# One head stage of a hybrid mLSTM and attention layer: values evicted by ScalarE, mLSTM steps one point sooner, low weight parts by VectorE at fixed places

## The chip, the cores and the metric

The kernel runs on one core of one Trainium2 chip. The metric is device time in microseconds, as the median of several runs. TensorE multiplies (PE in the profile, with PEld for the loading of its stationary operand), VectorE is DVE, ScalarE is ACT, GpSimd is POOL, and SyncE (SP) issues most of the DMAs.

## The reference

One decoder layer on 1024 tokens of width 1024 in float32. What the change touches is the middle of it, one mLSTM head and one attention head of each of three groups at a time:

```
proj = h @ w_in[l]
xc = silu(causal_depthwise_conv(xa, w_conv[l], b_conv[l]))
q_m, k_m = xc_h @ w_q_mlstm[l], xc_h @ w_k_mlstm[l] * DH ** -0.5
h_m = sigmoid(oa) * mlstm_chunkwise(q_m, k_m, v_m, ia + b_igate, fa + b_fgate)
h_m = rms_norm(h_m, g_mlstm_head[l]) + skip_mlstm[l] * xc
y_m = (h_m * silu(za)) @ w_out_mlstm[l]
...
outs, lses = dilated_window_attention(qh, kh, vh, window, dilation)   # three groups
o_a = sum(softmax(lses) * outs)
y_a = (o_a * silu(zb)) @ w_out_attn[l]
```

There are 4 mLSTM heads of width 256, and 3 attention groups of 4 heads of width 128 (windows 128, 512, 2048; dilations 1, 4, 16).

## The kernel before

Each engine runs its own hand-written program, in order, and semaphores tie them together. The program has stages: setup, blocks (projections as sums of block products), `mix` (the four heads), and merge (output projections and the final norm). The change is in `mix` alone.

**Float32 in three passes.** Every weight chunk of 128x1024 is split into a high part (ACT copies it to a rounded type, `whi`) and a low part (`wraw - whi` into `wlo`, by POOL at L1239). A product is three matmuls: high by high, high by low, low by high (L590 to L592). The semaphore `w_high` counts the high parts, `w_split` the low parts. SP loads chunk q into `wraw[q % 2]` once the low part of chunk q-2 is done (`load`, L1142 to L1145). PE starts with a chunk once its low part is done.

**A head** has eight chunks, p = 0 to 7. p = 0, 1, 3, 4 are the token projections n = 0 to 3 (v and the output gate, 48 matmuls each, in `project_tokens`); p = 2 is the fold chunk (`fw`, the products of the q and k weights); p = 5, 6, 7 are n = 4, 5, 6 (ZA twice and ZB, 48 matmuls each, in `project`). So n = 2 needs the low part of p = 3. Call T the time at which PE begins n = 0 of a head.

**Points.** The 144 matmuls of n = 4, 5, 6 are cut into 24 parts of six, and behind each part (`point` u = 0 to 23) PE does a step of mLSTM and a step of attention. `SCORES`, `ATTEND`, `NORM` and `TURN` say at which u they begin. An mLSTM chunk takes two steps: `state_update` and `scores_and_keys` at the even one, `numerator` at the odd one. An attention group takes six steps x = 0 to 5: `turn_values` at x = 0, scores at x = 0 to 3, transposed probabilities (`p_turned`) at x = 1 to 4, products with the values at x = 2 to 5. ACT and DVE have a `mixing(u)` of their own. On DVE it does `head_out` (odd mLSTM step) or `state` and `weigh` (even step), then attention: the masks of the scores (L1739) and the copy of the transposed probabilities into `pT` (L1748, L1751). Behind u = 20 come `head_norm`, and behind the turned output `head_scaled`, `silu_za`, and then the next head's `conv(0)`.

**Around a head's start** DVE does: conv(0); the sigmoid gate of the previous head's z (`silu_zb`); `weigh_groups`, which waits once for ACT's exp; conv_gate(0); conv(1); conv_gate(1); the low parts of xc; the scaling and joining of the previous head's three attention outputs; `fold_low`; `intra_args`.

Of the kernel before, what the change touches and what calls it, by code (L numbers as in the profile page):

```python
# [9 lines left out]
P = 128  # L10
# [240 lines left out]
def buffers(sb, ctx, table):  # L251
# [28 lines left out]
    ("hin", [P, DH + 1], F32), ("hnb", [P, DH + 1], F32), ("small", [P, 4], F32), ("vr", [P, 6, NCH], F32), ("nm", [P, 2, 2], F32),  # L280
# [788 lines left out]
def mix(nc, a, sem, ps, T):  # L1069
# [52 lines left out]
    SCORES, ATTEND, NORM, TURN = 4, 3, 20, 23  # L1122
# [110 lines left out]
    def gpsimd(pool):  # L1233
        for q in range(HEAD0, MERGE0 + 2 * PLAIN):
            p = (q - HEAD0) % CHUNKS
            at = q % 2 if q >= MERGE0 else ring_slot((q - HEAD0) // CHUNKS, p - (p > FOLD))
            hi, to = (fw[:, 0, :], fw[:, 1, :]) if p == FOLD and q < MERGE0 else (whi[:, at, :], wlo[:, at, :])
            pool.wait_ge(w_high, q - 2)
            nc.gpsimd.tensor_tensor(to, wraw[:, q % 2, :], hi.bitcast(F32), ALU.subtract).then_inc(w_split, 1)  # L1239
# [5 lines left out]
    def tensor(pe):  # L1245
        t_ = nc.tensor
        for i in range(0, HEADS):
# [103 lines left out]
            def turn_output():  # L1351
                for j in range(4):
                    pe.wait_ge(normed, 2 * i + 2 + j // 2)
                    if j == 3:
                        pe.wait_ge(out_used, i * 4 + 5)
                    for c in range(4):
                        mm = t_.transpose((M0, M1, M2, M0)[j][:, c * P:(c + 1) * P],
                                          og[:, 4 * (j // 2) + c, (j % 2) * P:(j % 2 + 1) * P], ident[:])
                    mm.then_inc(out_turned, 1)
# [72 lines left out]
    def scalar(act):  # L1432
# [4 lines left out]
        for i in range(0, HEADS):  # L1437
# [78 lines left out]
            def intra_weights():  # L1516

                act.wait_ge(e_arg, i + 1)
                for c in range(NCH):
                    ins = A(ew[:, c, :], ew[:, c, :], ACT.Exp, bias=hc[:, i, 0, c:c + 1])  # L1520
                ins.then_inc(e_exp, 1)
# [21 lines left out]
            def root_table():  # L1543
                act.wait_ge(normed, 2 * i + 1)
                A(vr[:, 2, 0:1], one[:], ACT.Abs_reciprocal_sqrt).then_inc(root_done, 1)

            def attend(g, x):
                if x >= 2:
# [12 lines left out]
            def mixing(u):  # L1561
                m, at = mlstm_step(u), attend_step(u)
                if u == NORM - 1:
                    root_table()
                if m is not None and m % 2:
                    inter((m - 1) // 2)
                if at:
                    attend(*at)
                if m is not None and m % 2:
                    square((m - 1) // 2)  # L1570
# [17 lines left out]
            next_high(5)  # L1588
            fold_high()
            for j in range(4):  # L1590
                keep_tokens(0, j)
            for n in range(ZA, MAIN):
                for h in range(2):
                    for part in range(PARTS_OF):
# [4 lines left out]
                        if (n, h, part) == (ZA, 0, 1):  # L1599
                            for j in range(4):  # L1600
                                head_keep(j)
# [6 lines left out]
                        if u == NORM + 1:  # L1608
                            z_sigmoid(ZA)
                            z_sigmoid(ZA + 1)  # L1610
# [4 lines left out]
    def vector(dve):  # L1615
# [10 lines left out]
        for i in range(0, HEADS):  # L1626
            hp = hpa[:, i]

            def conv(q):
                dve.wait_ge(xa_in, 16 * i + 16)  # L1630
                if q:
                    dve.wait_ge(xc_done, i * 2 + 1)
                x = xa[:, q, :]
# [26 lines left out]
            def weigh(c):  # L1660
                dve.wait_ge(sk_out, i * 8 + c + 1)
                if c == 0:
                    dve.wait_ge(e_exp, i + 1)
# [29 lines left out]
            def head_norm():  # L1693
# [9 lines left out]
                for h in range(2):  # L1703
                    cs = slice(4 * h, 4 * h + 4)
                    v.tensor_tensor(og[:, cs], og[:, cs], vr[:, 5, cs].unsqueeze(2).broadcast_to([P, 4, DH]), ALU.mult).then_inc(normed, 1)  # L1705
                for q in range(2):
                    step(v.tensor_scalar(xc[:, q, :], xc[:, q, :], hp[:, q, 5:6], None, ALU.mult))

            def head_scaled():
                for j in range(4):  # L1710
# [3 lines left out]
                    v.scalar_tensor_tensor(part_, (M0, M1, M2, M0)[j], hp[:, q, 6:7], part_, ALU.mult, ALU.add).then_inc(out_used, 1)  # L1714

            def silu_za(q):
                dve.wait_ge(z_sig, i * 3 + q + 1)
                z = (cv, sg)[q]
                step(v.tensor_tensor(z[:], z[:], tn[1 - q], ALU.mult))
                if q == 0:  # L1720
                    dve.wait_ge(out_used, i * 4 + 8)
                v.tensor_tensor(xc[:, q, :], xc[:, q, :], z[:], ALU.mult).then_inc(um_done, 1)
# [5 lines left out]
            def attend(g, x):  # L1728
                if x == 0:
                    for j in range(2):  # L1730
                        dve.wait_ge(v_turned, i * 6 + 2 * g + j + 1)
                        v.tensor_copy(vt[:, 4 * j:4 * j + 4, :], (A1, A2)[j].rearrange("p (c e) -> p c e", c=4)).then_inc(v_kept, 1)  # L1732
# [62 lines left out]
            def mixing(u):  # L1795
                m, at = mlstm_step(u), attend_step(u)
                if m is not None and m % 2:
# [17 lines left out]
            conv_gate(0)  # L1815
            conv(1)
            conv_gate(1)
# [4 lines left out]
            if i:  # L1822
                scale_two(i - 1)
                join_two(i - 1)
                join_third(i - 1)
# [6 lines left out]
            silu_za(0)  # L1832
            silu_za(1)
# [532 lines left out]
```

## Time and profile before

| | |
|---|---|
| Time, median of 3 runs | 1391.75 us (1391.37 to 1392.53) |
| Profiled execution: time | 1391.71 us |
| Profiled execution: span | 1389.7 us |
| PE busy | 1354.6 us, 97% |
| DVE busy | 863.7 us, 62% |
| ACT busy | 561.1 us, 40% |
| POOL busy | 448.3 us, 32% |
| The head stage | about 575 to 1119 us |

The span is what the profiler saw of the core's work, and the time of that execution is 2.0 us more. The granted PE clock is full (2.4 GHz) in all 40 slices of the page, and the mean over the span is 0.999. A matmul's end is modelled, so durations of neighbours overlap: a 128x512 matmul is listed at 0.39 us, and the next starts 0.23 us after it. Where an interval is wanted, the starts are to be read.

### The profile page before, as it was taken

The page shows a single profiled execution, that of the slowest core. Times are in us where ns is not written, and L with a number is a line of the kernel's source. Part 1 is how long each engine was busy: PE and PEld are TensorE (multiplying, and loading weights), DVE is VectorE, ACT ScalarE, POOL GpSimd, SP SyncE. Part 2 cuts the span into 40 slices and gives each one's busy share as a digit, 9 for nine tenths or more (in the row PEclk, how much of TensorE's full clock was granted, in tenths as well). Part 3 has the DMA queues.
Part 4 walks back from the last instruction along what each step waited for, and adds up shares of the span by engine and source line. Part 5 has one row for each costly group of instructions (what it writes and reads, how often), then busy time and mean ns, then how long its engine had stood idle before and what let it go on. Part 6 is the DMA issues. An engine that isn't in the chain of part 4 may idle for free.

```text
span 1389.7 us, 17404 instructions
## 1 busy us (share of the span) xinstructions
PE 1354.6 (97%) x6477; PEld 1132.2 (81%) x6477; DVE 863.7 (62%) x1474; ACT 561.1 (40%) x980; POOL 448.3 (32%) x288
## 2 busy tenths in 40 slices
PE   8999999999999999999999999999999899999998
PEld 6888888888888888888877887888788787888886
DVE  7888765664734554345677567665866566433586
ACT  7664343344444444234343434444444335111122
POOL 0196555454544555420022002200220021222551
PEclk9999999999999999999999999999999999999999
DMA  8512322332324433462218311730272056354543
GB/s 333 190 62 101 129 108 105 122 121 94 118 101 142 152 137 139 168 177 59 52 47 232 89 30 48 242 92 16 76 213 61 17 204 236 107 179 154 178 137 106
DMA packets 64334, 176.31 MB, mean 127 GB/s; under 512 B 21906, under 2 KB 22034, under 8 KB 62199
## 3 DMA queue, kind: packets, MB, share of 16 engines
q1 hardware_dynamic: 59962, 162.44, 35.2%
q10 hardware_dynamic: 3168, 8.70, 1.9%
q0 software_dynamic: 1120, 4.06, 1.0%
q8 instruction: 52, 0.85, 0.3%
q14 instruction: 32, 0.25, 0.1%
HBM read 130.39 MB, written 44.79 MB: 126 GB/s over the span
## 4 chain that ended last, share of the span: by engine, by line
PE 83%; DVE 8%; ACT 4%; DMA 4%; issue 1%; SPq 0%; POOL 0%; ACTq 0%; DVEq 0%
PE banks L590 24%; PE banks L592 24%; PE banks L591 24%; DMA wraw<-in_w_all 3%; PE banks L1391 2%; PE banks L1381 1%; PE banks L1341 1%; PE banks L1347 1%; PE banks L1400 1%; PE banks L582 1%; PE banks L554 1%; ACT whi L1465 1%; PE banks L1339 1%; DVE vt L1732 1%; DVE og L1705 1%
## 5 line engine op out<-in xcount | busy, mean ns | idle before, releaser
L590 PE MATMUL banks<-h_hi,whi 128*128 128x512 f32 x584 | 234.9, 402 | 0.0
L1239 POOL TENSOR_TENSOR wlo<-wraw,whi 128x1024 fp32r<-128x1024 f32 x32 | 78.1, 2442 | 485.4 <-ACT whi L1465 458.3
L592 PE MATMUL banks<-h_hi,wlo 128*128 128x512 f32 x584 | 228.1, 391 | 0.0
L591 PE MATMUL banks<-h_lo,whi 128*128 128x512 f32 x584 | 227.6, 390 | 0.0
L714 POOL TENSOR_TENSOR wlo<-w_sum,whi 128x512 fp32r<-128x512 f32 x104 | 154.4, 1487 | 127.1 <-ACT whi L839 127.1
L590 PE MATMUL banks<-t_hi,whi 128*128 128x512 f32 x416 | 161.8, 389 | 0.0
L591 PE MATMUL banks<-t_lo,whi 128*128 128x512 f32 x416 | 161.8, 389 | 0.0
L592 PE MATMUL banks<-t_hi,wlo 128*128 128x512 f32 x416 | 161.8, 389 | 0.0
L985 DVE TENSOR_TENSOR c_sum<-c_sum,banks 128x512 f32<-128x512 f32 x182 | 124.8, 686 | 42.5 <-PE banks L592 29.7
L592 PEld LDWEIGHTS banks<-h_hi,wlo 128*128 128x128 f32 x584 | 109.6, 188 | 23.5
L839 ACT ACTIVATE whi<-w_sum 128x512 fp32r<-128x512 f32 x104 | 65.4, 630 | 153.9 <-PE banks L592 93.1
L591 PEld LDWEIGHTS banks<-h_lo,whi 128*128 128x128 f32 x584 | 109.9, 188 | 20.5
L590 PEld LDWEIGHTS banks<-h_hi,whi 128*128 128x128 f32 x584 | 109.8, 188 | 20.4
L590 PE MATMUL banks<-whi,h_hi 128*128 128x512 f32 x256 | 99.9, 390 | 0.0
L592 PE MATMUL banks<-whi,h_lo 128*128 128x512 f32 x256 | 99.7, 389 | 0.0
L591 PE MATMUL banks<-wlo,h_hi 128*128 128x512 f32 x256 | 99.6, 389 | 0.0
L592 PEld LDWEIGHTS banks<-t_hi,wlo 128*128 128x128 f32 x416 | 78.1, 188 | 16.2
L590 PEld LDWEIGHTS banks<-t_hi,whi 128*128 128x128 f32 x416 | 78.1, 188 | 16.2
L591 PEld LDWEIGHTS banks<-t_lo,whi 128*128 128x128 f32 x416 | 78.1, 188 | 16.1
L861 ACT ACTIVATE fin<-c_sum 128x1024 f32<-128x1024 f32 x52 | 75.5, 1501 | 2.6 <-DMA chunk_decay_rows<-wlast 2.6
L714 POOL TENSOR_TENSOR wlo<-wraw,whi 128x512 fp32r<-128x512 f32 x39 | 58.2, 1500 | 44.7 <-ACT whi L839 44.7
L714 POOL TENSOR_TENSOR wlo<-raw,whi 128x512 fp32r<-128x512 f32 x39 | 54.7, 1414 | 47.6 <-ACT whi L839 47.6
(369 smaller groups left out, 2682.9 us busy)
## 6 DMA issues: line engine op xcount, KB each, us to landing
wraw<-in_w_all SPq DMA_DIRECT2D x74, 512.0 KB, 4.4
raw<-in_w_all SPq DMA_DIRECT2D x26, 512.0 KB, 4.4
queries_keys<-fin SPq DMA_DIRECT2D x12, 1024.0 KB, 4.0
qa<-queries_keys SPq DMA_DIRECT2D x12, 768.0 KB, 12.6
s_wada<-in_w_ada_cols SPq DMA_DIRECT2D x16, 512.0 KB, 6.8
attn_values<-fin SPq DMA_DIRECT2D x6, 1024.0 KB, 4.0
tn<-attn_values SPq DMA_DIRECT2D x12, 512.0 KB, 9.4
sig_c<-merge_gates SPq DMA_DIRECT2D x6, 1024.0 KB, 7.0
```

What stands on the lines that cost most here:

```text
L554: t_.matmul(to[:, h, :], w_hi, hi, start=(k == 0), stop=False)
L582: mm = t_.matmul(to[:, h, :], w_hi, h_lo[:, k, h * HALF:(h + 1) * HALF], start=False, stop=(k == KT - 1))
L590: t_.matmul(out, w_hi, x_hi, start=first, stop=False)
L591: t_.matmul(out, w_hi, x_lo, start=False, stop=False)
L592: return t_.matmul(out, w_lo, x_hi, start=False, stop=last)
L714: nc.gpsimd.tensor_tensor(wlo4[:, (o + 2) % 4, :], source(r, j), whi4[:, (o + 2) % 4, :].bitcast(F32), subtract).then_inc(s_split, 1)
L839: A(whi4[:, (o + 2) % 4, :], source(r, j), ACT.Copy).then_inc(s_high, 1)
L861: A(fin[r % 2][:, j, :].rearrange("p (r u) -> p r u", r=d), c_sum[:, r % 2, j, :].rearrange("p (u r) -> p r u", r=d), ACT.Sigmoid if r < Q ...
L985: v.tensor_tensor(out, x, bank(r, j), ALU.add).then_inc(part_added, 1)
L1239: nc.gpsimd.tensor_tensor(to, wraw[:, q % 2, :], hi.bitcast(F32), ALU.subtract).then_inc(w_split, 1)
L1339: mm = t_.matmul(M1[:, 0:DH + 1], sw[:, c % 2, :], v1[:, c, 0:DH + 1], start=True, stop=True)
L1391: mm = t_.matmul(A2[:, u * P:(u + 1) * P], vt[:, t + 1 - b + j, :], pT[:, u, j, :], start=(j == 0), stop=(j == b - 1))
```

## The change

1. `SCORES` goes from 4 to 3, `NORM` from 20 to 19, `TURN` from 23 to 22: mLSTM, the head's norm and the turning of its output come one point sooner. Attention stays.
2. The turned values are copied to `vt` by ACT, not by DVE (six copies of 128x512 a head).
3. The low parts of the heads' weights are made by DVE (`weights_low`), at places written in the order: p = 2 behind conv_gate(0), p = 3 behind conv(1), p = 4 behind `scale_two`, p = 5 behind `join_two`, p = 6, 7, 8 at u = 1, 8, 17 (`LOWS`), p = 9 (chunk n = 1 of the next head) behind `gate_out`. POOL keeps four of 36.
4. On DVE the pT copy of x = 4 comes ahead of the mLSTM step of its point; the scaling of xc by the skip weights comes at u = 18, ahead of head_out; the silu of z comes at u = 21 (`gate_silu`), with ACT's sigmoids at u = 20.
5. The fourth turned piece of the output goes to bank A0, not back to M0, so it no longer waits for `head_scaled`.
6. On ACT `next_high(5)` comes behind `keep_tokens(0, ...)`; the exp table is loaded ahead (`exp_table`); the root table is loaded behind the attention step of u = 18; the eight exps of `ew` signal one by one.

```diff
-    SCORES, ATTEND, NORM, TURN = 4, 3, 20, 23
+    SCORES, ATTEND, NORM, TURN = 3, 3, 19, 22
+
+    LOWS = {1: 6, 8: 7, 17: 8}
...
     def gpsimd(pool):
-        for q in range(HEAD0, MERGE0 + 2 * PLAIN):
...
+        for q in (HEAD0, HEAD0 + 1, MERGE0 + 2, MERGE0 + 3):
+            at = q % 2
             pool.wait_ge(w_high, q - 2)
-            nc.gpsimd.tensor_tensor(to, wraw[:, q % 2, :], hi.bitcast(F32), ALU.subtract).then_inc(w_split, 1)
+            pool.wait_ge(w_split, q + 2)
+            nc.gpsimd.tensor_tensor(wlo[:, at, :], wraw[:, q % 2, :], whi[:, at, :].bitcast(F32), ALU.subtract).then_inc(w_split, 1)
...
                     if j == 3:
-                        pe.wait_ge(out_used, i * 4 + 5)
+                        pe.wait_ge(masked, i * 24 + 25)
...
+            def weights_low(p):
+
+                q = HEAD0 + i * CHUNKS + p
+                r = p % CHUNKS
+                if r == FOLD:
+                    hi, to = fw[:, 0, :], fw[:, 1, :]
+                else:
+                    at = ring_slot(i + p // CHUNKS, r - (r > FOLD))
+                    hi, to = whi[:, at, :], wlo[:, at, :]
+                dve.wait_ge(w_high, q - 2)
...
+                v.tensor_tensor(to, wraw[:, q % 2, :], hi.bitcast(F32), ALU.subtract).then_inc(w_split, 1)
...
             def mixing(u):
                 m, at = mlstm_step(u), attend_step(u)
+                if u == NORM - 1:
+                    skip_scaled()
+                if at and at[1] == 4:
+                    attend(*at)
                 if m is not None and m % 2:
                     head_out((m - 1) // 2)
...
-                if at:
+                if at and at[1] != 4:
                     attend(*at)
                 if u == NORM:
                     head_norm()
+                if u == TURN - 1:
+                    gate_silu()
+                if u in LOWS:
+                    weights_low(LOWS[u])
...
             conv_gate(0)
+            weights_low(FOLD)
             conv(1)
+            weights_low(3)
             conv_gate(1)
...
-            silu_za(0)
-            silu_za(1)
+            gate_out(0)
+            gate_out(1)
+            weights_low(CHUNKS + 1)
```

**VectorE at the start of a head.** `fw` is the fold chunk, `xc` the gated convolution, `cv` the convolution. Before:

```order
L1644 TENSOR_TENSOR xc<-cv,sg 128x1024 [waits um_out0,conv_sig,dve_steps]
L1634 TENSOR_SCALAR cv<-xa,hpa 128x1024 [waits xc_done,xa_in]
L1636 SCALAR_TENSOR_TENSOR cv<-xa,hpa,cv 128x1024 [waits dve_steps] x3
L1644 TENSOR_TENSOR xc<-cv,sg 128x1024 [waits um_out1,conv_sig]
L1648 TENSOR_TENSOR xc_lo<-xc,xc_hi 128x1024 [waits xc_high_done] x2
```

Now (heads 1 to 3), where the second L1650 row is the low part of p = 3:

```order
L1669 TENSOR_TENSOR xc<-cv,sg 128x1024 [waits um_out0,conv_sig,dve_steps]
L1650 TENSOR_TENSOR fw<-wraw,fw 128x1024 [waits w_high]
L1659 TENSOR_SCALAR cv<-xa,hpa 128x1024 [waits xc_done,xa_in]
L1661 SCALAR_TENSOR_TENSOR cv<-xa,hpa,cv 128x1024 [waits dve_steps] x3
L1650 TENSOR_TENSOR wlo<-wraw,whi 128x1024 [waits w_high]
L1669 TENSOR_TENSOR xc<-cv,sg 128x1024 [waits um_out1,conv_sig]
L1673 TENSOR_TENSOR xc_lo<-xc,xc_hi 128x1024 [waits xc_high_done] x2
```

Two low parts moved in from POOL, one on either side of conv(1).

**TensorE from u = 7 to u = 8** (the last transposed probabilities of group 0, the six matmuls of a part, then mLSTM). `sm` are the probabilities; `sw` and `kw` come from DVE's `weigh`. Before:

```order
L1400 MATMUL banks<-ident,sm 128x128 x3
L590 MATMUL banks<-h_hi,whi 128x512 [waits kept0,w_split]
L591 MATMUL banks<-h_lo,whi 128x512
L592 MATMUL banks<-h_hi,wlo 128x512
L590 MATMUL banks<-h_hi,whi 128x512
L591 MATMUL banks<-h_lo,whi 128x512
L592 MATMUL banks<-h_hi,wlo 128x512
L1347 MATMUL banks<-v,kw 128x257 [waits num_kept]
```

Now:

```order
L1401 MATMUL banks<-ident,sm 128x128 x3
L590 MATMUL banks<-h_hi,whi 128x512 [waits kept0,w_split]
L591 MATMUL banks<-h_lo,whi 128x512
L592 MATMUL banks<-h_hi,wlo 128x512
L590 MATMUL banks<-h_hi,whi 128x512
L591 MATMUL banks<-h_lo,whi 128x512
L592 MATMUL banks<-h_hi,wlo 128x512
L1340 MATMUL banks<-v,sw 128x257 [waits state_done,sw_done]
```

Behind the six matmuls PE now asks for DVE's `state` and `weigh` of this point, where it asked for `num_kept` of the point before.

**VectorE at u = 17 and 18** (end of the last attention group). `nm` and `pT` belong to attention, `hnb` to mLSTM. Now:

```order
L1774 COPY pT<-banks 128x2x128 [waits p_turned]
L1650 TENSOR_TENSOR wlo<-wraw,whi 128x1024 [waits w_high]
L1734 TENSOR_SCALAR xc<-xc,hpa 128x1024
L1734 TENSOR_SCALAR xc<-xc,hpa 128x1024 [waits dve_steps]
L1700 TENSOR_TENSOR hnb<-banks,hin 128x257 [waits gated,inter_kept,dve_steps]
```

A low part and the scaling of xc now stand between a pT copy and the last head_out; before, nothing did.

## Rows read from the trace of the kernel before

**Rows 1.** Page, part 4: the chain that ended last, share of the span by engine

```profile
PE 83%; DVE 8%; ACT 4%; DMA 4%; issue 1%; SPq 0%; POOL 0%; ACTq 0%; DVEq 0%
```

**Rows 2.** Waits of PE from 560 to 1150 us: total, times, longest

```profile
PE banks L1391 <- DVE pT L1748: 4.6, 4, 1.2
PE banks L1357 <- DVE xc L1714: 4.3, 4, 1.1
PE banks L1381 <- DVE st L1739: 4.2, 4, 1.1
```

**Rows 3.** Timeline of PE, head 1: start, duration, engine, line, operation, [idle before <- releaser]

```profile
710.88 0.48 PE L590 MATMUL banks<-whi,h_hi 128*128 128x512 f32 x1
...
754.53 0.28 PE L590 MATMUL banks<-fw 128*128 128x256 f32 x1
...
760.45 0.47 PE L590 MATMUL banks<-xc_hi,fold 128*128 128x512 f32 x1 [1.59 <-ACT og L1459]
...
782.10 0.60 PE L1400 MATMUL banks<-ident,sm 128*128 128x128 f32 x4
...
783.93 0.59 PE L1339 MATMUL banks<-v,sw 128*128 128x257 f32 x2
...
823.32 0.68 PE L1381 MATMUL banks<-qa 128*128 128x128 f32 x4 [1.06 <-DVE st L1739]
...
832.98 0.68 PE L1391 MATMUL banks<-pT,vt 128*128 128x128 f32 x4 [1.02 <-ACT ew L1553]
...
840.00 0.71 PE L1391 MATMUL banks<-pT,vt 128*128 128x128 f32 x4 [1.16 <-DVE pT L1748]
...
847.22 0.63 PE L1357 MATMUL banks<-ident,og 128*128 128x128 f32 x4 [1.07 <-DVE xc L1714]
```

**Rows 4.** Timeline of DVE in the points of head 1

```profile
782.74 0.69 DVE L1748 COPY pT<-banks 128x512 f32<-128x512 f32 x1 [0.28 <-PE banks L1400]
...
789.40 0.86 DVE L1690 SCALAR_TENSOR_TENSOR cst<-cst,dec,banks 128x257 f32<-128x257 f32 x2
...
790.38 0.47 DVE L1666 TENSOR_SCALAR kw<-banks,hc 128x256 f32<-128x256 f32 x1
...
828.02 0.43 DVE L1675 TENSOR_TENSOR hnb<-banks,hin 128x257 f32<-128x257 f32 x1 [2.27 <-ACT hin L1528]
...
829.53 0.15 DVE L1735 COPY small<-zero 128x1 f32<-128x1 f32 x1
```

**Rows 5.** Timeline of DVE, start of head 1 (last row: end of head 1)

```profile
708.03 1.54 DVE L1707 TENSOR_SCALAR xc<-xc,hpa 128x1024 f32<-128x1024 f32 x2
...
712.25 3.35 DVE L1719 TENSOR_TENSOR cv<-cv,tn 128x1024 f32<-128x1024 f32 x1
...
719.17 0.81 DVE L1634 TENSOR_SCALAR cv<-xa,hpa 128x1024 f32<-128x1024 f32 x1
...
727.56 0.94 DVE L1763 TENSOR_TENSOR cw<-cw,ct 128x24 f32<-128x24 f32 x1 [1.98 <-ACT cw L1537]
...
732.12 3.93 DVE L1636 SCALAR_TENSOR_TENSOR cv<-xa,hpa,cv 128x1024 f32<-128x1024 f32 x3
...
738.31 1.22 DVE L1648 TENSOR_TENSOR xc_lo<-xc,xc_hi 128x1024 fp32r<-128x1024 f32 x1
...
842.47 2.36 DVE L1705 TENSOR_TENSOR og<-og,vr 128x1024 f32<-128x1024 f32 x2
```

**Rows 6.** Timeline of POOL, start of head 1: a low part

```profile
712.14 2.38 POOL L1239 TENSOR_TENSOR fw<-wraw,fw 128x1024 fp32r<-128x1024 f32 x1
```

**Rows 7.** Timeline of DVE, head 0: the start of conv(1)

```profile
593.39 2.71 DVE L1634 TENSOR_SCALAR cv<-xa,hpa 128x1024 f32<-128x1024 f32 x1
```

**Rows 8.** Timeline of ACT, end of head 1: an eviction, then the root table

```profile
835.51 0.60 ACT L1449 ACTIVATE szb<-banks 128x512 f32<-128x512 f32 x1 [0.48 <-PE banks L592]
836.13 1.28 ACT L1545 ACT_TABLE_LOAD   x1
```

**Rows 9.** DMAs of L1145 (weight chunks): issue to landing, us

```profile
DMA to landing us min/median/max: 3.5/4.5/13.5
```

More of the change, by code:

```diff
@@ L1519, in intra_weights, with exp_table @@
                 for c in range(NCH):
-                    ins = A(ew[:, c, :], ew[:, c, :], ACT.Exp, bias=hc[:, i, 0, c:c + 1])
-                ins.then_inc(e_exp, 1)
+                    A(ew[:, c, :], ew[:, c, :], ACT.Exp, bias=hc[:, i, 0, c:c + 1]).then_inc(e_exp, 1)
+            def exp_table():
+                act.wait_ge(normed, 2 * i + 1)
+                A(small[:, 5:6], one[:], ACT.Exp)
             def inter(c):
@@ L1544, in root_table @@
                 act.wait_ge(normed, 2 * i + 1)
-                A(vr[:, 2, 0:1], one[:], ACT.Abs_reciprocal_sqrt).then_inc(root_done, 1)
+                A(small[:, 4:5], one[:], ACT.Abs_reciprocal_sqrt).then_inc(root_done, 1)
             def attend(g, x):
+                if x == 0:
+                    for j in range(2):
+                        act.wait_ge(v_turned, i * 6 + 2 * g + j + 1)
+                        A(vt[:, 4 * j:4 * j + 4, :], (A1, A2)[j].rearrange("p (c e) -> p c e", c=4), ACT.Copy).then_inc(v_kept, 1)
                 if x >= 2:
@@ L1627, in vector @@
             hp = hpa[:, i]
+            def weights_low(p):
[7 more added lines that the diff above has]
+                dve.wait_ge(w_high, q - 2)
+                if p == FOLD and i == 0:
+                    dve.wait_ge(w_split, q + 2)
+                v.tensor_tensor(to, wraw[:, q % 2, :], hi.bitcast(F32), ALU.subtract).then_inc(w_split, 1)
             def conv(q):
@@ L1632, in conv @@
                     dve.wait_ge(xc_done, i * 2 + 1)
+                elif i:
+                    dve.wait_ge(um_done, i * 2 - 1)
                 x = xa[:, q, :]
@@ L1713, in head_scaled, with gate_silu, gate_out @@
                     part_ = xc[:, q, h * HALF:(h + 1) * HALF]
[L1714 to L1719, printed above, removed]
+                    v.scalar_tensor_tensor(part_, (M0, M1, M2, A0)[j], hp[:, q, 6:7], part_, ALU.mult, ALU.add).then_inc(out_used, 1)
+            def gate_silu():
+                for q in range(2):
+                    dve.wait_ge(z_sig, i * 3 + q + 1)
+                    z = (cv, sg)[q]
+                    step(v.tensor_tensor(z[:], z[:], tn[1 - q], ALU.mult))
+            def gate_out(q):
                 if q == 0:
                     dve.wait_ge(out_used, i * 4 + 8)
-                v.tensor_tensor(xc[:, q, :], xc[:, q, :], z[:], ALU.mult).then_inc(um_done, 1)
+                v.tensor_tensor(xc[:, q, :], xc[:, q, :], (cv, sg)[q][:], ALU.mult).then_inc(um_done, 1)
             def silu_zb(j):
@@ L1728, in attend @@
             def attend(g, x):
[L1729 to L1732, printed above, removed]
                 if x < 4:
@@ L1823, in vector @@
                 scale_two(i - 1)
+            weights_low(4)
+            if i:
                 join_two(i - 1)
+            weights_low(5)
+            if i:
                 join_third(i - 1)
```

19 lines of the change are left out of this document (9 added, 10 removed).

## The prediction

> **What bounds the kernel.** The chain that ended last is PE for 83% [rows 1], so time is saved only where PE stands still. I read the page first, then PE's waits in the head stage [rows 2], then PE's timeline in one head [rows 3], and DVE's, ACT's and POOL's at the same places. The reader is to see that three kinds of wait come four times each, once a head, at 1.1 to 1.2 us, always at the same places, and that DVE, though only 62% busy, ends most of them: it is late at a few points, not full.
>
> **What goes.** A wait costs PE about 0.17 us more than the idle time shown, because listed matmuls overlap; I read starts. In head 1 [rows 3]: 823.32, scores behind DVE's masks, 1.25 us; with the exp behind them another 0.5; 832.98, a bank that ACT can't empty because `weigh` of the last chunk comes late, 1.2, and 0.15 behind it; 840.00, a pT copy queued behind head_out, 1.35; 847.22, the fourth turned piece, 1.25; and 0.3 at u = 10. That is 5.9 a head.
> - Masks: the value copies (two of 128x512) leave DVE and mLSTM is a point ahead, so DVE's masks are done some 2 us before PE asks. Gone.
> - Bank: `weigh(7)` comes at u = 17, a whole point before PE's next use. Gone.
> - pT copy: at u = 19 no mLSTM step is left on DVE. What is late there now is counted below.
> - Turned piece: A0 waits only for masks long done. Gone.
>
> Four heads give 23.6, and 0.2 more in head 0. The start of `head_q` in head 1 waited 1.6 for ACT's evictions (at 760.45) [rows 3], which stood behind a high part that waited for its DMA; that high part now stands behind them. 0.3 us of it stays (what two other heads show), so this gives 1.5, and 0.2 in head 3. **Removed: 25.5 us.**
>
> **What comes, 1: the points u = 8 and u = 14.** DVE takes the pT copy of x = 4 ahead of its mLSTM step, and that step (state, then weigh) is one that PE now asks for six matmuls later. From the last transposed probability to a free numerator PE needs 1.5 us (782.43, the last of the four of the row at 782.10, to 783.93) [rows 3]. DVE needs 0.3 to start, 0.6 for the copy, and from 789.40 to 790.85 for state and weigh, 1.45 [rows 4]; with 0.1 for the semaphores 2.45. So PE waits 0.95 at u = 8, and 0.9 at u = 14, where the copy is a little smaller. In the order before, DVE's step was a point away from its use, and that cover is gone. **4 x 1.85 = 7.4 us.** Bounds: 0 if DVE's copy could overlap more, 1.2 each.
>
> **What comes, 2: the start of a head.** A low part costs DVE what L1648 costs, same form: 1.22 us, and 1.14 until the next can start [rows 5]. POOL's took 2.38 [rows 6]. But DVE ran no faster while POOL did: L1719 took 3.35 instead of 1.22 beside POOL's fold part [rows 5, 6], 2.1 lost; L1763 took 0.94 instead of 0.17, 0.77 lost. These come back.
>
> The question is when the low part of p = 3 is done, since PE starts n = 2 on it. T is 710.88, and four chunks end at 754.53, so n = 2 is due at T + 21.8 [rows 3]. Before, POOL made it beside conv(1) at no cost to PE. Now it stands behind conv(1), whose end was 736.05, T + 25.2 [rows 5]. I count in three steps from PE's last numerator, at u = 18, as zero.
> - To the norm (the og products, 842.47 before). DVE at u = 17 and 18 has a low part (1.14) and the scaling of xc (1.6 with its step) [rows 5] behind a pT copy, and is free at 2.1; head_out takes 1.5 (828.02 to 829.53 [rows 4]) to 3.6; the masks are read at 4.35 and the pT copy ends at 4.7. ACT's exps of them end at 5.25. The root table, loaded before in ACT's idle time (836.13, 1.28 us [rows 8]), now stands behind them: 6.55. The square (0.6), two evictions (0.8) and the root (0.2) end at 8.05. DVE's six small steps: og starts at 9.3. Before it was 7.15 behind the same numerator.
> - To conv(0). Before, 13.4 us (842.47 to 719.17 + 136.72, the period of a head [rows 5]). Now without the scaling (-1.6) and POOL's contention (-2.1), with a low part (+1.15): 10.9. So 20.2.
> - To the low part of p = 3. Before, conv(0) to the end of conv(1) took 16.9 (719.17 to 736.05). Now -0.8, + 1.15 for the fold part, + 1.2 for its own, 0.1 for the semaphore: 18.4. So 38.6.
>
> PE without any wait gets to n = 2 at 34.1: five points took 9.7 without their waits, a sixth is 2.6 more, and 21.8 follow. The excess is 4.4 us at each start of heads 1 to 3, **13.2 us**. In it is a wait of 0.95 at u = 19 for the pT copy (4.7 against 3.8) and one of about 0.85 at T, where PE asks for ACT's eviction of the product just finished (that was hidden behind the turning, which is now a point sooner); neither adds, since DVE sets the end. Head 0: conv(1) began at 593.39 [rows 7]; less 0.2, plus 1.15 for the fold part, 4.7 and 1.2: done at 600.3, against n = 2 due at 575.45 + 21.8 = 597.2. **3.1 us.** The end of head 3: 0.95 at u = 19 and 0.8 for the norm's second half, **1.75 us**; behind it POOL still makes the merge's parts and nothing moves. Further on the low part of p = 4 comes some 2 us before n = 3 wants it. SP's queue: the loads behind `load(p = 5)`, queries and values too, start 2 us later and are wanted 30 us later; nothing.
>
> Bounds of these chains: each may be 1 us shorter or 1.5 longer, since short steps add up, times four.
>
> **Sum.** Removed 25.5; added 7.4 + 13.2 + 3.1 + 1.75 = 25.5. Net 0 against the profiled execution (span 1389.7, time 1391.71, which is the median to 0.05). Forecast 1391.7.
>
> **A rule against a row.** ACT's root table: the row shows the load 0.02 us behind the eviction ahead of it (835.51 + 0.60) and 1.28 long [rows 8]. The Trainium skill, "ScalarE: Activation LUTs", "What ACT_TABLE_LOAD costs", gives about 1.28 us for the load and 1.38 for a drain at every switch. By that rule the chain above would be 1.4 longer in each head. The trace doesn't show such a drain as a gap ahead of the load.
>
> **Rivals.**
> - A, slower: the chunk p = 3 lands late. Its load is now issued by SP only behind the low part of p = 9, at conv(0) + 0.2, where POOL let it go before conv(0) began. ACT wants it at conv(0) + 5.8 and only then does its high part, the exp of `weigh_groups`, and DVE with them. Landings are 3.5 to 13.5, median 4.5 [rows 9], and two stores of xc follow it. From 5.6 us on, each further us costs three heads 1 us: at 7.1, 4.5 us, 1396.2. A lengthened DVE chain of any kind has the same price. Chance 0.22.
> - B, faster: the chains are shorter than my sums, or n = 2 waits half as long. With all of it gone (8.0 at three starts beyond the 1.75 that the end costs anyway, and 3.1) 1380.7; half of it, 1386.2. For it: DVE is idle for 2 us in `weigh_groups` and I let nothing fill that. Chance 0.20.
> - C: the table's switch costs 1.4 us more where it now stands, four times: 5.5 us, 1397.2. It would need idle time ahead of the load, which the rows don't have. It is the rule above. Chance 0.04.
> - D, the change doesn't take the values off the path: at u = 3 ACT has eight exps (2.4 us) and an eviction ahead of them, and PE's transposes wait for `vt`. I find 0 to 0.3 us of slack; if it is 1 us late in each head, 1395.7. Chance 0.06.
> - Forecast: 0.48, with its own range 1388.5 to 1395.
>
> **Numbers.** A measurement of this kernel can tell about 0.2% from no change, 2.8 us, so 1389.0 and 1394.5 are the bounds. Faster: 0.17 of B and 0.10 of the forecast, 0.27. Slower: 0.16 of A, C, 0.04 of D, 0.05 of the forecast, 0.29. Same: 0.44. The range 1386 to 1396.5 takes in half of B and A at its price, and leaves some 0.1 on either side.
>
> **What would show it.** PE's waits on DVE's st, ACT's ew and DVE's xc (L1714) should be gone from the list. A wait of 2 to 3 us four times on the new low part (L1650) at the first matmul of n = 2 shows step 2; if it is over 4, rival A; if it is missing, B. Two waits of 0.8 to 1.0 a head on DVE's kw at the numerator show step 1. DVE's L1747 at 1.22 instead of 3.35 shows the contention gone. What would make it wrong: a DVE chain misjudged by 1 us, which comes four times.

## The result, and the profile after

The changed kernel takes 1398.76 us (median of 6 runs, 1396.81 to 1399.73) beside 1392.14 us for the kernel before (6 runs): a ratio of 1.004, 95% interval 1.0027 to 1.0053. In a second series it took 1396.92 us beside 1392.18. So it is slower by 4.7 to 6.6 us, and both times lie above the forecast's range, which ended at 1396.5. The profiled execution took 1399.73 us with a span of 1397.9, 8.2 above the span of before. The second series was profiled too (span 1394.8); that is "the second execution" below.

PE is still the chain, for 86% instead of 83% [rows 1]. This is part 4 of the page of after, shares of the span by engine:

```profile
PE 86%; DVE 7%; ACT 2%; issue 2%; DMA 2%; SPq 0%; DVEq 0%; ACTq 0%
```

PE's waits in the head stage of after (total, times, longest) answer to [rows 2]:

```profile
PE banks L590 <- DVE wlo L1650: 8.4, 4, 3.0
PE banks L1340 <- DVE kw L1691: 5.8, 8, 0.8
PE banks L1392 <- ACT ew L1561: 3.7, 4, 0.9
PE banks L1392 <- DVE pT L1774: 3.7, 4, 0.9
PE banks L590 <- issue: 2.5, 3, 0.8
PE banks L590 <- ACT szb L1450: 0.8, 1, 0.8
```

The kinds that the prediction wanted gone are gone; the two with like names (ACT `ew` and DVE `pT`) now stand at other places. The first two rows were forecast, the last four in part. In PE's timeline they stand, for the end of head 1 and the start of head 2, like this (start, duration, ..., [idle before <- releaser]):

```profile
797.93 0.70 PE L1340 MATMUL banks<-v,sw 128*128 128x257 f32 x2 [0.76 <-DVE kw L1691]
...
843.40 0.71 PE L1392 MATMUL banks<-pT,vt 128*128 128x128 f32 x4 [0.93 <-DVE pT L1774]
...
846.75 0.68 PE L1392 MATMUL banks<-pT,vt 128*128 128x128 f32 x4 [0.92 <-ACT ew L1561]
...
854.13 0.47 PE L590 MATMUL banks<-whi,h_hi 128*128 128x512 f32 x1 [0.84 <-issue]
...
877.83 0.50 PE L590 MATMUL banks<-whi,h_hi 128*128 128x512 f32 x1 [1.65 <-DVE wlo L1650]
```

Read by starts, as in the prediction, these are 0.95 at a numerator, 1.10 at u = 19, 1.11 at u = 20, 1.02 at T and 1.82 ahead of n = 2. The last is 23.7 us behind T (854.13 to 877.83).

DVE's timeline in the same stretch: the low part of p = 8 and the scaling at u = 17 and 18, L1747 without contention, conv(0), the wait for `ct`, the wait for ACT's exp, the low part of p = 3.

```profile
838.04 1.22 DVE L1650 TENSOR_TENSOR wlo<-wraw,whi 128x1024 fp32r<-128x1024 f32 x1
839.17 1.54 DVE L1734 TENSOR_SCALAR xc<-xc,hpa 128x1024 f32<-128x1024 f32 x2
...
850.26 1.23 DVE L1747 TENSOR_TENSOR cv<-cv,tn 128x1024 f32<-128x1024 f32 x1
...
858.95 0.81 DVE L1659 TENSOR_SCALAR cv<-xa,hpa 128x1024 f32<-128x1024 f32 x1
...
866.12 0.17 DVE L1785 TENSOR_TENSOR cw<-ct 128x8 f32<-128x8 f32 x1 [1.25 <-DMA ct<-softmax_stats]
...
867.97 0.18 DVE L1789 TENSOR_TENSOR cw<-cw,ct 128x24 f32<-128x24 f32 x1 [1.26 <-ACT cw L1541]
...
876.55 1.22 DVE L1650 TENSOR_TENSOR wlo<-wraw,whi 128x1024 fp32r<-128x1024 f32 x1
```

ACT's: the root table and the two evictions behind it, then the high part of p = 3, the exp table, the exp of `weigh_groups`.

```profile
843.75 0.18 ACT L1566 ACTIVATION_READ_ACCUMULATOR sm<-sm,nm 128x1 f32 x1
843.95 1.28 ACT L1549 ACT_TABLE_LOAD   x1
...
845.75 0.57 ACT L1450 ACTIVATE szb<-banks 128x512 f32<-128x512 f32 x1
846.23 0.37 ACT L1561 ACTIVATE ew<-banks 128x256 f32<-128x256 f32 x1
...
865.34 1.06 ACT L1466 ACTIVATE whi<-wraw 128x1024 fp32r<-128x1024 f32 x1 [0.51 <-PE banks L592]
866.41 1.28 ACT L1541 ACT_TABLE_LOAD   x1
867.71 0.22 ACT L1541 ACTIVATE cw<-cw 128x24 f32<-128x24 f32 x1
```

SP's queue at the start of head 1, the DMAs that it issues, of before and then of after, and DVE's wait there in after:

```profile
716.89 2.71 SPq L1178 DMA_DIRECT2D mlstm_branch<-xc  x2
719.65 0.43 SPq L1180 DMA_DIRECT2D ct<-softmax_stats  x1
```

```profile
720.67 0.36 SPq L1147 DMA_DIRECT2D wraw<-in_w_all  x1
721.07 0.91 SPq L1180 DMA_DIRECT2D mlstm_branch<-xc  x2
722.02 1.39 SPq L1182 DMA_DIRECT2D ct<-softmax_stats  x1
```

```profile
729.22 0.17 DVE L1785 TENSOR_TENSOR cw<-ct 128x8 f32<-128x8 f32 x1 [2.76 <-DMA ct<-softmax_stats]
```

The kernel before doesn't have one thing inside the heads: PE was granted 1.2 GHz instead of 2.4 for 3.4 us behind the wait ahead of n = 2 in heads 0 and 1. Such a stretch is called a fall of the clock below. The windows of after (PE, PEld, DVE, ACT and POOL busy, granted clock, DMA share, GB/s) and a run of matmuls at the lower level, in head 1:

```profile
601.00:605.00 4.00, 3.26 (x8) 2.64 (x9) 4.00 (x4) 2.64 (x3) 0.00 (x0) 0.57 0.57 178
738.00:741.00 3.00, 1.04 (x5) 0.86 (x6) 3.00 (x3) 1.27 (x2) 0.00 (x0) 1.00 0.73 255
741.00:745.00 4.00, 4.00 (x12) 3.17 (x11) 3.42 (x4) 1.79 (x2) 0.00 (x0) 0.57 0.96 310
```

```profile
739.96 0.50 PE L590 MATMUL banks<-whi,h_hi 128*128 128x512 f32 x1 [2.16 <-DVE wlo L1650]
...
742.89 0.63 PE L590 MATMUL banks<-whi,h_hi 128*128 128x512 f32 x1
743.32 0.63 PE L591 MATMUL banks<-wlo,h_hi 128*128 128x512 f32 x1
```

Starts are 0.43 us apart there against 0.23 at full clock, so the eight matmuls of such a stretch, 3.4 us, cost 8 x 0.2 = 1.6 to 1.7 us. The profiled execution has a third fall, at 28 us in the setup stage.

### The profile page after: what moved, and what is told of

It is laid out like the page before. It is cut to its first block, busy times and chain, and to the rows that moved or that the text cites. A ratio compares the mean times of both kernels' runs of the same rounds, so it can differ in the third digit from the quotient of the medians.

```text
span 1397.9 us, 17450 instructions
## 1 busy us (share of the span) xinstructions
PE 1358.9 (97%) x6477; PEld 1134.9 (81%) x6477; DVE 847.6 (61%) x1482; ACT 575.3 (41%) x1008; POOL 370.8 (27%) x256
## 4 chain that ended last, share of the span: by engine, by line
PE 86%; DVE 7%; ACT 2%; issue 2%; DMA 2%; SPq 0%; DVEq 0%; ACTq 0%
PE banks L590 24%; PE banks L592 24%; PE banks L591 24%; PE banks L1392 2%; PE banks L1382 2%; PE banks L1342 1%; PE banks L1348 1%; DVE cv L1661 1%; PE banks L1340 1%; PE banks L1331 1%; PE banks L1401 1%; PE banks L554 1%; PE banks L582 1%; DVE wlo L1650 1%; PE banks L1370 1%
## 5 line engine op out<-in xcount | busy, mean ns | idle before, releaser
L1240 POOL TENSOR_TENSOR wlo<-wraw,whi 128x1024 fp32r<-128x1024 f32 x4 | 10.6, 2642 | 573.8 <-ACT whi L2047 566.2
L590 PEld LDWEIGHTS banks<-whi,h_hi 128*128 128x128 f32 x256 | 48.8, 191 | 23.9 <-DVE wlo L1650 10.1
```

The costliest lines, as they stand in the source:

```text
L590: t_.matmul(out, w_hi, x_hi, start=first, stop=False)
```

## The experiments

Times are set beside runs of the kernel before on the same chip, which took 1392.92 us in the first series (four kernels), 1392.60 in the second (four), 1391.5 in the third (three), 1392.18 in the fourth (two) and 1393.25 in the fifth (three). Each kernel's name stands beside its time.

**Where the low part of p = 3 stands.** Two kernels moved it alone:

```diff
             weights_low(FOLD)
+            weights_low(3)
             conv(1)
-            weights_low(3)
             conv_gate(1)
```

> The changed kernel with one line moved: the low part of p = 3 ahead of conv(1), not behind it. Theory W (time is the sum of TensorE's waits, and a wait of over 2 us at n = 2 is followed by a fall of the clock): the waits at the first matmul of n = 2 (3.1, 2.3, 1.8, 1.8 us, 9.1 together) go, and with them the two falls of the granted clock at 601 and 741 us (1.7 us each): 12.5 us off the changed kernel, about 1386 against the 1392 of the kernel before. Rival K (the falls of the clock have nothing to do with the wait): 9.1 us off, about 1389.5, and falls still in the head stage. Rival D (VectorE as a whole is too full, and the wait only moves): a new wait at n = 3 or at head_q of 1 to 3 us in each head, little gain.

`low3_early` measured 1389.02 us, ratio 0.9967 (0.9955 to 0.9979). The waits ahead of n = 2 and both falls in the heads are gone, and all other waits are as they were. The time alone can't tell the theories apart: 1389.02 is rival K's figure, but K wanted the falls to stay. The profiled spans, each with one fall in the setup stage, are 11.5 apart, where theory W says 12.5. The other kernel put it behind `conv_gate(1)`:

```diff
-            weights_low(3)
             conv_gate(1)
+            weights_low(3)
```

> The changed kernel with the low part of p = 3 one step later, behind conv_gate(1). Theory W: each of the four waits at n = 2 grows by 1.15 us, to 4.3, 3.5, 3.0 and 3.0; heads 2 and 3, whose waits were 1.8 and showed no fall of the clock, now show one too, 1.7 us each: 4.6 + 3.4 = 8 us above the changed kernel, about 1406.5. Rival K (falls are independent of the wait): 4.6 us above, about 1403.5, with as many falls as before.

`low3_late` measured 1413.41 us, ratio 1.0141 (1.0125 to 1.0156): more than either expected. The wait row:

```profile
PE banks L590 <- DVE wlo L1650: 17.8, 4, 5.1
```

It grew by 9.4 in four heads, not by 4.6, since DVE waits for ACT's sigmoid ahead of it (1.12 us each), and the clock fell in all four heads, in head 0 for 6.8 us. So this place is on the path, at full price in both directions.

**The pT copy and the numerators.**

```diff
-                if at and at[1] == 4:
+                if at and at[1] == 4 and m is None:
                     attend(*at)
```

(and the reverse condition behind the mLSTM step)

> The changed kernel with VectorE's pT copy of x = 4 behind state and weigh again at u = 7 and u = 13 (at u = 19, where there is no mLSTM step, nothing changes). Theory W: the waits at the numerators of u = 8 and u = 14 (0.95 and 0.87 us, eight in all) go, and no other appears, since the copy is wanted only a numerator later: 7.2 us off, about 1391.5. Rival: the copy then comes late for the value product of u = 8 and 14, and the wait only moves: no gain, 1398.5.

`pt_order` measured 1391.05 us, ratio 0.9991 (0.9981 to 1.0). The eight numerator waits are gone and no other wait takes their place: step 1 was right in size and place. (In head 1 the wait ahead of n = 2 is 2.73 here instead of 2.34, since `ct` landed later still.)

**Part 3 apart from the other parts.** The changed head order with every low part by POOL, as before:

```diff
-        for q in (HEAD0, HEAD0 + 1, MERGE0 + 2, MERGE0 + 3):
+        for q in range(HEAD0, MERGE0 + 2 * PLAIN):
...
-                if u in LOWS:
-                    weights_low(LOWS[u])
```

> The changed kernel with part 3 undone: all low parts of the heads' weights by GpSimd again, all else as changed. Theory W: the waits at n = 2 go (9.1 us and two clock falls, 3.4), VectorE is 1.1 us earlier at u = 18 but still has the scaling of xc there, so the wait at u = 19 goes to about 0; 12.5 + 4 = 16 us off, about 1382. VectorE's operations beside GpSimd's are stretched again (1.2 to 2.1 us each), which costs TensorE only where VectorE is awaited: at most 3 us. Rival D (the low parts on VectorE are not what costs): within 3 us of 1398.5.

`after_poollow` measured 1385.13 us, ratio 0.9944 (0.993 to 0.9959). No wait ahead of n = 2, no fall in the heads. And the order before, with part 3 alone at the same places:

```diff
     SCORES, ATTEND, NORM, TURN = 4, 3, 20, 23
+    LOWS = {1: 6, 8: 7, 17: 8}
...
+            weights_low(FOLD)
             conv(1)
+            weights_low(3)
             conv_gate(1)
```

> The kernel before with part 3 alone: low parts by VectorE at the same places, all else as before. Theory S: conv(0) starts at T + 7.3 (8.3 before, 2.1 less by GpSimd's contention, 1.1 more by a low part), so the low part of p = 3 ends at T + 26 and n = 2 waits 4.3 us in heads 1 to 3 and 3.1 in head 0, 16 us, each with a clock fall (1.7, 6.8 together); at u = 16 the wait for the masks loses 1.2 us of contention, at u = 18 the one for weigh gains 1: about 22 us above the kernel before, 1414. Rival (the low parts on VectorE cost nothing by themselves, the mLSTM shift does): within 4 us of 1392.

`before_dvelow` measured 1411.24 us, ratio 1.0125 (1.0097 to 1.0153). Its first rows of PE's waits:

```profile
PE banks L590 <- DVE wlo L1642: 15.4, 5, 3.5
PE banks L1392 <- ACT ew L1554: 7.2, 4, 1.8
```

So all parts but the third are worth 7.8 us together, and low parts by VectorE cost 18.6 alone, with four falls of the clock in it. On top of the other parts they cost 11.8 to 13.6 (1396.92 and 1398.76 against 1385.13, on different chips). How the 7.8 us divide among parts 1, 2, 4, 5 and 6 wasn't tried.

**Are the waits ahead of T absorbed?** Two kernels loosened one thing ahead of T each: the skip product behind `head_norm` instead of at u = 18, and the root table behind the value eviction.

```diff
-                if u == NORM - 1:
-                    skip_scaled()
...
                 if u == NORM:
                     head_norm()
+                    skip_scaled()
```

> The changed kernel with the scaling of xc behind the head's norm again (behind the og products at u = 19), not at u = 18 ahead of head_out. Theory S (VectorE's chain from u = 17 to the low part of p = 3 sets the start of heads 1 to 3, waits inside it don't add): the wait of 1.1 us at u = 19 goes in all four heads, but VectorE has the same work up to conv(0), so n = 2 waits by as much longer; only head 3's end keeps a gain: 1 to 1.5 us off the changed kernel, about 1397, maybe plus clock falls behind longer waits at n = 2 in heads 2 and 3 (+3.4). Rival A (waits add up one by one): 4.4 off, about 1394.

`skip_late` measured 1401.26 us, ratio 1.0062 (1.0042 to 1.0082). Both theories wanted the wait at u = 19 gone, and it only shrank by 0.2, to 0.88. DVE's head_out of u = 18, in head 1, says why:

```profile
841.93 0.43 DVE L1700 TENSOR_TENSOR hnb<-banks,hin 128x257 f32<-128x257 f32 x1 [1.28 <-ACT hin L1532]
```

DVE stood still for 1.28 us there, for ACT's eviction (L1532) of the numerator that PE had just made. With all low parts by POOL (`after_poollow`, `pool_pt_root`) the wait at u = 19 is still 0.92. So 0.2 of the 1.10 us is the work that was put ahead of head_out, and 0.9 is the way of a numerator from PE over ACT to DVE and back as a pT copy.

The wait ahead of n = 2 grew in heads 2 and 3 from 1.82 to 2.69. 1.54 us more in DVE's chain behind the norm cost 0.87 there, so that chain had about 0.7 us of slack; beyond it DVE's chain sets n = 2, as theory S has it.

```diff
-                if u == NORM - 1:
-                    root_table()
                 if m is not None and m % 2:
                     square((m - 1) // 2)
                 if u == NORM:
+                    root_table()
                     rstd()
```

> The changed kernel with ScalarE's root table loaded at u = 19, behind the eviction of the value product, not at u = 18 ahead of the square and that eviction. The wait of 1.1 us at u = 20 (TensorE for that eviction) goes. Theory S: VectorE's norm starts no earlier, so in heads 1 to 3 the gain comes back as a longer wait at n = 2; about 1 us off, 1397 to 1398, or more clock falls. Rival A: 4.4 off, about 1394.

`root_late` measured 1397.67 us, ratio 1.0038 (1.0022 to 1.0053). The wait at u = 20 is gone, and 0.6 us comes at the turning, which waits for og. In heads 2 and 3 the wait ahead of n = 2 is 1.82 as in the changed kernel, 23.67 us behind T (855.60 to 879.27). So the 0.5 us a head that are saved ahead of T are kept, not absorbed (from T of head 2 to T of head 3 it is 135.72 us instead of 136.24): within the slack theory S is wrong. In head 1 the wait was 3.16, since `ct` landed late. The time doesn't show the gain: it was eaten in the profiled execution by that wait and by longer falls of the clock (6.8 us each in heads 0 and 1).

**All four orders at once**, and then three of them without the later skip product:

> The changed kernel with all four moves: low part of p = 3 ahead of conv(1), pT copy of x = 4 behind state and weigh where there is an mLSTM step, scaling of xc behind the norm, root table behind the eviction at u = 19. If the waits are all there is: of 28.9 us of waits some 4 remain (TensorE at the start of heads, for ScalarE's eviction of the product just finished), no clock fall in the heads: 25 + 3.4 off the changed kernel, 1370. Rival (a next bound behind them, VectorE as a whole): 1377 or more.

`all4` measured 1385.11 us, ratio 0.9935 (0.9919 to 0.9951), 15 above the first expectation. Some of the waits stayed: 0.9 at u = 19 in each head, for the reason above. New ones came: one ahead of n = 3, 1.4 us in each of heads 1 to 3, 1.5 at the merge's second chunk, and a smaller one at the turning as in `root_late`. The low part of p = 4 stands behind the longer DVE chain, and the skip product had lengthened that.

> Three of the four orders together, without the later skip product: VectorE's low part for the third chunk ahead of conv(1), the copy of the turned probabilities behind the mLSTM step, ScalarE's root table behind the value eviction. Theory W, each takes away its own waits and nothing else: from the 1389.0 us of the first alone, minus 4 x (0.95 + 0.88) for the numerators, minus 4 x (1.1 - 0.37 - 0.26) for the table: 1379.8 us, and the 1.4 us wait at the fourth chunk that the run of all four shows is gone, since the skip product in the chain ahead of it brought it. Rival C, VectorE's chain from the merge to the fourth chunk is full in any such order: the wait of 1 to 1.5 us at the fourth chunk stays in heads 1 to 3 and at the end of head 3, and the time is 1383 to 1385 us.

`early_pt_root` measured 1379.56 us, ratio 0.991 (0.9894 to 0.9925), 0.2 from the first theory. Of the wait ahead of n = 3 only 0.8 us in head 1 is left. The same with the low parts by POOL:

> The changed order of the heads with all low parts back on GpSimd (measured 1385.1 us), and the probabilities' copy behind the mLSTM step and ScalarE's root table behind the value eviction. Theory W: minus 4 x 1.83 and minus 4 x 0.47 from 1385.1: 1375.9 us, no fall of the clock inside the heads. Rival C, VectorE shares its time with GpSimd at other places once the chain is 2 us shorter in each head, and half of the gain is given back: 1379 to 1381 us.

`pool_pt_root` measured 1376.74 us, ratio 0.9889 (0.9874 to 0.9904): 15 us faster than the kernel before, and the best of all. The first rows of its list of waits:

```profile
PE banks L1393 <- DVE pT L1774: 3.0, 4, 0.8
PE banks L590 <- issue: 2.5, 3, 0.8
PE banks L1359 <- DVE og L1730: 0.9, 4, 0.2
```

**What the falls of the clock cost.** PE's waits ahead of n = 2 filled with matmuls:

```diff
+                if n == VO + 2 and s == 0:
+                    for _ in range((11, 8, 6, 6)[i]):
+                        t_.matmul(ps[0:1, TOKEN_BANKS[0], :], zero[:, 0:1].bitcast(F32R), h_hi[:, 0, 0:HALF], start=False, stop=False)
                 pe.wait_ge(w_split, chunk(i, n) + 3)
```

> The changed kernel with work that fills TensorE's wait ahead of the third chunk's token tiles: 11, 8, 6 and 6 matmuls of 512 columns in heads 0 to 3, with a weight of zeros, added to a bank that is in use (so they add nothing to the result). 11 of 0.213 us are 2.3 us of the 3.17 us wait, 8 are 1.7 of 2.34, 6 are 1.3 of 1.82, so none of the waits should end later. Theory F, TensorE's idleness in these waits is what the granted clock falls behind: both stretches at half clock inside the heads go, and with them 2 x 1.7 us, time 1395.4 us. Rival N, the falls come there whatever TensorE does and the price of the waits is the wait itself: the falls stay, 1398.8 us. If filling costs more than it hides: above 1399.5.

`filler` measured 1396.39 us, ratio 1.0031 (1.002 to 1.0041). There is no fall in the heads. The starts in the filling are 0.23 us apart in the trace, not 0.213, so 11 of them take 2.5 us; n = 2 still begins no later than without them, 24.8 us behind T in head 0 (24.9 in the changed kernel). The filling and what follows, in head 0, and the window that answers to the first above:

```profile
598.75 2.71 PE L1286 MATMUL banks<-h_hi,zero 128*1 128x512 f32 x11
601.81 0.51 PE L590 MATMUL banks<-whi,h_hi 128*128 128x512 f32 x1 [0.35 <-DVE wlo L1653]
602.15 0.40 PE L591 MATMUL banks<-wlo,h_hi 128*128 128x512 f32 x1
```

```profile
601.00:605.00 4.00, 3.65 (x16) 2.66 (x15) 4.00 (x4) 2.72 (x3) 0.00 (x0) 1.00 0.55 167
```

Both kernels again on one chip:

> The changed kernel once more, unchanged, beside the one with TensorE's waits filled, on one chip. The earlier pair ran on two chips: 1398.76 us and 1396.39 us, 2.4 apart, while their profiled spans were 3.3 apart. Theory F, the falls of the granted clock behind the waits cost 3.4 us: 1398 to 1399.5 us here, 2.5 to 3.4 above the other, and both falls in the profile. Rival N: within 1 us of the other.

`after_again` measured 1396.92 us, ratio 1.0037 (1.0024 to 1.0049).

> The changed kernel with 11, 8, 6 and 6 matmuls by a weight of zeros in TensorE's waits ahead of the third chunk, once more. Theory F: 1395 to 1396.5 us, 2.5 to 3.4 below the unfilled one, no fall inside the heads. Rival N, the 2.4 us between the earlier pair were the two chips: within 1 us of the unfilled one.

`filler_again` measured 1396.65 us, ratio 1.0029 (1.0017 to 1.0042). By the medians rival N holds, 0.3 us. The traces say why it can't be read so: the unfilled kernel's profiled execution (span 1394.8) had a fall in head 0 only and a wait of 1.82 in head 1, and the filled one's had a fall in the setup stage, at 28 us, where neither kernel differs. So the single times say more than the medians. In the two series of the filled kernel five of 13 lie from 1395.04 to 1395.30 and the others from 1396.28 up; of the 11 of the unfilled kernel the lowest five lie from 1396.61 to 1397.05. The lowest are 1.6 us apart (1395.04 and 1396.61), which is one fall by the spacing of the starts.

That PE's idleness brings the falls in the heads is shown: the two filled kernels have none in any head, and the unfilled ones have one in head 0 in both profiles. How many an execution has besides varies, so the share in the median, 0.3 to 2.4 us, isn't settled.

**What sets the wait ahead of n = 2.** The second execution had the lead: it is 23.7 us from T to n = 2 in heads 1 to 3. So it is in heads 2 and 3 of the first, of `pt_order` and of `root_late`; in `skip_late`, with more work behind the norm, it is 24.5. A constant distance from T points to a chain that starts with PE's own work. ACT may write the high part of p = 3 when PE has done n = 0 (865.34, released by PE, T + 11.2); then its exp table (1.28) and exp; then DVE's 9.8 us from 867.97 to the low part's end. Three kernels tested it. The first moves only SP's issues: stores of xc and the load of `ct` ahead of the weight load that waits for DVE's low part.

```diff
+            load(HEAD0 + i * CHUNKS + 7 + AHEAD)
             sp.wait_ge(cw_done, i + 1)
...
-                load(HEAD0 + i * CHUNKS + p + AHEAD)
+                if p < 7:
+                    load(HEAD0 + i * CHUNKS + p + AHEAD)
```

> The changed kernel with one thing moved on SP's queue: the two stores of xc and the load of the softmax statistics (ct) go ahead of the load of the weight chunk that waits for VectorE's last low part of the head. Theory P, the wait at the third chunk is set by TensorE's own end of the first chunk (11.2 us behind the head's start, when ScalarE may write the high part, then its table and exp, then 9.9 us of VectorE): the waits of heads 2 and 3 stay at 1.82 us, that of head 1 falls from 2.34 to 1.82, time 0.5 us less, or 2.2 with one fall of the clock less. Theory D, VectorE's chain from the last head's norm sets it, with the late ct in it: all three waits shrink by 1.2 us or more, 4 us less.

`ct_first` measured 1396.72 us, ratio 1.0033 (1.0023 to 1.0043). DVE doesn't wait for `ct` any more (the first row has no idle time), and waits longer for the exp, which hangs on PE and ACT. DVE's rows, then ACT's, at the start of head 2:

```profile
863.82 0.16 DVE L1787 TENSOR_TENSOR cw<-ct 128x8 f32<-128x8 f32 x1
...
867.03 0.18 DVE L1791 TENSOR_TENSOR cw<-cw,ct 128x24 f32<-128x24 f32 x1 [2.63 <-ACT cw L1543]
```

```profile
864.39 1.06 ACT L1468 ACTIVATE whi<-wraw 128x1024 fp32r<-128x1024 f32 x1 [0.54 <-PE banks L592]
865.48 1.28 ACT L1543 ACT_TABLE_LOAD   x1
866.77 0.23 ACT L1543 ACTIVATE cw<-cw 128x24 f32<-128x24 f32 x1
```

The waits ahead of n = 2 are 1.82, 1.82 and 1.82, as theory P had it. The second kernel swaps two steps on ACT:

```diff
-            next_high(2)
             if i:
                 group_exp(i - 1)
+            next_high(2)
```

> The changed kernel with ScalarE's exp of the group weights ahead of its high part of the third chunk. Theory P: in heads 2 and 3 the exp comes as soon as ct is there and its differences are made (12.8 us behind the head's start instead of 13.6), the waits at the third chunk fall from 1.82 to about 1.0; head 1, where ct comes last, stays. Time 1.6 us less. Theory D: no change.

`exp_first` measured 1398.41 us, ratio 1.0033 (1.0021 to 1.0046). The waits of heads 2 and 3 fell to 0.71 and 0.97, that of head 1 stayed at 2.31. The gain of 2 us doesn't show in the time. The profiled execution had a fall of twice the length in head 0, 1.7 us more, and it wasn't alone in that: the mean granted clock is 0.995 or 0.996 in all five executions, and 0.997 or 0.998 in eight of the nine of `ct_first`. Why the falls are longer here is open. Both together:

> Both together. Theory P: with ct there earlier and the exp not behind the high part, ScalarE's table load behind its sigmoid sets it, 1.6 us sooner: the waits at the third chunk of heads 1 to 3 fall to about 0.2 us, the fall of the clock in head 1 goes, and the time is 5 to 7 us less than the changed kernel's, 1391 to 1393.5 us. Theory D: 4 us less, from ct alone, so no better than ct alone.

`exp_ct_first` measured 1392.81 us, ratio 0.9996 (0.9987 to 1.0005), 4 us below the kernel with `ct` alone on the same chip. Of this row only head 0's wait is left:

```profile
PE banks L590 <- DVE wlo L1652: 2.9, 1, 2.9
```

With the exp no longer tied to PE's first chunk and `ct` there in time, the waits of heads 1 to 3 are gone: `ct` alone gave 0.5 in head 1 and nothing in heads 2 and 3, the exp alone 1.0 in the mean of heads 2 and 3 and nothing in head 1, both together all of it. They are two conditions side by side, and the later one counts.

## Why the prediction was wrong

In short: the waits that the change brings were sized at 25.5 us and measured 29.3, and the falls of the clock behind the longest of them, 3.4 us in the profiled execution, stood in no term. By the prediction's own steps, each wait read by starts:

- **Removed, 25.5 us: right** (the terms of its 5.9 a head, as rounded, add to 6.0). None of the waits of [rows 2] and [rows 3] is left, and L1747 takes 1.23 instead of 3.35 [rows 5]. From T of head 2 to T of head 3 it is 135.25 us before and 136.24 after; less the waits between, 5.9 and 6.9, it is 129.35 in both.
- **Step 1, numerators, 7.4: right.** 8 waits, 7.3 in sum, and moving the copy removes them.
- **Head 0, 3.1: right.** 3.17 in the profiled execution, 3.00 in the other.
- **The starts of heads 1 to 3, 13.2: too low, 15.7.** As a sum it was near. From the last numerator to the low part of p = 3 DVE's chain took 39.3 us where 38.6 was said: 9.4 to the og products (847.94) for 9.3, 11.0 to conv(0) for 10.9, 18.8 to the low part for 18.4, whose own terms add to 18.55. PE without its waits took 34.3 where 34.1 was said. So the excess is 5.05 instead of 4.4, and 5.57 in head 1, where `ct` landed late. The prediction's 4.4 is 0.95 at u = 19, 0.85 at T and the rest, 2.6, ahead of n = 2; measured are 1.10, 1.11 at u = 20, 1.02 at T and 1.82.
- **The step that failed is "neither adds, since DVE sets the end".** Ahead of its last piece DVE stands still for 1.26 us for an exp that hangs on the end of PE's n = 0. The prediction had that stretch in its 18.4 as if it were DVE's own work. It fixes n = 2 at T + 23.7, 1.82 behind its due time, as long as DVE's work behind the norm isn't more than 0.7 us longer (`skip_late`). So the waits at u = 19 (1.10), u = 20 (1.11) and T (1.02) add to it. `root_late` shows it for the wait at u = 20, `ct_first` and `exp_ct_first` for the exp.
- **The wait at u = 19, 0.95: right in size (1.10), by luck in the reason.** It was put down to DVE's low part and scaling. They are 0.2 of it, as `skip_late` shows.
- **The wait at u = 20 was missed.** PE asks there for ACT's eviction of the value product (846.23), which stands behind the root table (843.95), a square and another eviction. The prediction counted that table on the way to the norm and not for this second customer of ACT's queue. `root_late` removes the wait.
- **The end of head 3, 1.75: too low, 3.15**, by the missed wait and 0.2 on the others.
- **SP's queue: half wrong.** Apart from rival A the prediction put it at nothing. But the weight load at a head's end waits for DVE's low part, and behind it on SP stand not only the stores of xc but the load of `ct`. It was issued 0.5 us behind the start of conv(0) before (719.65, [rows 5]) and 1.5 behind it after (722.02; conv(0) at 720.56), behind three transfers issued within 1.4 us, and DVE had it 7.2 us later (before, it landed 2.5 us behind its issue). In head 1 of the profiled execution that made n = 2 wait 0.5 more. Rival A spoke of a late chunk p = 3 instead; that one didn't happen, and that its price for a longer chain gives 1396.2, near the result, is luck.
- **The clock.** 3.4 us of the profiled execution are two falls of PE's clock behind the waits ahead of n = 2, one in the second execution. No term of the sum had them. `low3_early` and the filled kernels are without them.

Added, then: 7.3 + 3.2 + 15.7 + 3.15 = 29.3 instead of 25.5, 3.8 more. With 3.4 for the two falls and 1.4 for the fall in the setup stage, which the change doesn't touch (T of head 0 is 576.82 instead of 575.45), it makes 8.6 against 8.2 in the spans; 0.4 isn't placed. For the second execution it is 3.1 + 1.7 = 4.8 against 5.1. On rival C the result says nothing for it: the table load stands 0.02 us behind ACT's record ahead of it (843.75 and 0.18, then 843.95), so here too the trace doesn't show, as a gap, the drain that the Trainium skill, "ScalarE: Activation LUTs", "What ACT_TABLE_LOAD costs", adds to each switch.

## What to carry to other kernels

Before a wait is called absorbed, follow the late chain back to its last release: if it starts again from the waiting engine's own work (here a buffer that PE frees), what stands ahead of that point isn't absorbed, until the other chain (here 0.7 us shorter) becomes the later one. When a step joins an in-order queue, list all later customers of that queue, DMA queue included, with what each is wanted for. And when a table load or an exp stands behind a step that waits for another engine, swap them first: with `ct` in time that gave 4 us here. Time the parts of a change apart: all but the third part here, with two small orders more, gave 15 us over the kernel before.

## What the runs showed of the hardware

All of this is of the waits of PE ahead of n = 2. The granted clock fell to 1.2 GHz behind those of 3.0 us and more in every profile, and behind those of 2.3 to 2.7 us sometimes: it did at 2.34 (head 1 of the changed kernel), 2.73 (head 1 of `pt_order`) and 2.69 (head 1 of `skip_late`), and not at 2.31 (head 1 of `exp_first`) or at 2.69 in heads 2 and 3 of `skip_late`. Behind 1.82 it never did, in 12 waits. Matmuls by a weight of zeros, one column wide, kept it at 2.4 GHz, as the filled windows show. A wait that long thus costs up to 1.7 us, sometimes 3.4, beyond itself.

Idle waits aren't all of it. Ten of the 18 profiles have a fall at 28 to 29 us, in the setup stage, with no idle time of PE over 0.6 us in the 10 us ahead of it; its cause is open.
